# The first MLP matrix by Strassen's seven half products, in a fp32 decoder trunk on one core

## The chip, the core and the metric

The kernel runs on one core of a Trainium2 chip. The core has a matrix engine, TensorE (PE in the profile, its weight loads PEld), three engines for elementwise work, VectorE (DVE), ScalarE (ACT) and GpSimd (POOL), and SyncE (SP), which here only issues loads. Each engine works through its own queue in order; they meet at semaphores. Matmuls write to PSUM banks of 512 fp32 columns; everything else lies in SBUF. The metric is the device time of one execution in microseconds (us), as the median of several.

## The reference

A trunk of two layers over 512 tokens of width 1024. Each layer adds a mixer of four branches, then cross attention, then the MLP, which is the part that changes:

```python
def sq_relu_mlp(h, w1, w2):
    return jnp.square(jax.nn.relu(h @ w1)) @ w2
...
    for l in range(DEPTH):
...
        h = rmsnorm(x, norm_mlp[l])
        x = x + sq_relu_mlp(h, mlp_w1[l], mlp_w2[l])
```

`w1` is 1024 x 4096 and `w2` 4096 x 1024, all in fp32.

## The kernel before

**Layout.** Activations lie turned: a tile is 128 features (partitions) by 512 tokens (columns), eight of them for width 1024. `X` is the residual stream, `Hhi`/`Hlo` the normed input. fp32 products are made of three: every operand is split into a high part and a low part (fp32r), and the matmuls are high x high, high x low and low x high.

**Units.** Weights come in units of 256 x 256 numbers: 128 partitions by two row blocks (`k`) by 256 columns. SP loads each unit into a ring of nine places (`WR`, in the trace `w_raw`), when PE has used the unit nine before it. For each unit ACT writes the high part (`feed`, L1327, `w_hi`), then POOL the low part over the raw one in two instructions of 256 columns (L637 and L638, `w_lo`), then PE may use it (`split_ready`). `feed_past(name)` lets ACT go LEAD = 5 units beyond a block.

**Blocks.** A block makes 256 output features from 1024 input features: 4 units, in each 2 output tiles (`reg`) x 2 input tiles (`k`) x 3 matmuls of 512 columns, 48 matmuls in all. Blocks take turns between two sets of two PSUM banks (`G`); a block may start when both banks of the block before last are released: `pe.wait_ge(gemm_free[s], 2 * used)` at the head of `parts`. The reader of a bank releases it with an empty instruction (`dve.nop().then_inc(gemm_free[s], 1)`). Four more banks, `M` (in the trace `mix`), serve the mixer and the attention.

**The MLP.** `up{q}_{c}` is quarter q (of 1024 hidden features), column c (256 of them); `down{q}_{c}` multiplies quarter q by `w2` and adds to `X`. PE's order is up0, up1, down0, up2, down1, up3, down2, down3, four blocks each (`block_order`). DVE reads an `up` bank with relu and the norm factor in one instruction into `gate_t` (the trace shows `gate_t<-gemm,work`, L1835), ACT squares it (L1798) and writes the high part (L1799), DVE the low part (`work_split<-gate_t,work_split`). A `down` bank is added to `X` by DVE (`x_t<-x_t,gemm`, L1826, in `residual`). The hidden quarters lie in `work_split`, in two places in turn (`MHID`). Elementwise steps go through `do`, by which an engine waits for its own last instruction before it starts the next. `factors(2)` makes the norm's factor from a matmul at the end of `up0_0`, so DVE starts on the MLP at 656.1 us in the first layer.

## Time and profile before

| | |
|---|---|
| median of 3 runs (lowest, highest) | 1979.01 us (1978.82, 1979.11) |
| the profiled execution, its span | 1979.01 us, 1977.2 us |
| PE busy | 1954.3 us (99%) |
| DVE, ACT, POOL busy | 959.0 (49%), 913.8 (46%), 1086.8 us (55%) |
| PE clock granted in the 40 slices | 9 or more tenths in all |
| HBM traffic | 95 GB/s over the span |

The page gives busy time by engine, then the span in 40 slices, the chain of work that ended last, and the costliest groups of instructions with their mean durations. The trace of the same execution can be asked for the instructions of a stretch in order of time, for who waited for whom, and for busy time by stretch. Matmuls overlap one another, so their pace is read from the distance of their starts and not from their durations. All times are from the start of the span.

### The profile page before, as it was taken

The page shows a single profiled execution, that of the slowest core. Times are in us where ns is not written, and L with a number is a line of the kernel's source. Part 1 is how long each engine was busy: PE and PEld are TensorE (multiplying, and loading weights), DVE is VectorE, ACT ScalarE, POOL GpSimd, SP SyncE. Part 2 cuts the span into 40 slices and gives each one's busy share as a digit, 9 for nine tenths or more (in the row PEclk, how much of TensorE's full clock was granted, in tenths as well). Part 3 has the DMA queues.
Part 4 walks back from the last instruction along what each step waited for, and adds up shares of the span by engine and source line. Part 5 has one row for each costly group of instructions (what it writes and reads, how often), then busy time and mean ns, then how long its engine had stood idle before and what let it go on. Part 6 is the DMA issues. An engine that isn't in the chain of part 4 may idle for free.

```text
span 1977.2 us, 30720 instructions
## 1 busy us (share of the span) xinstructions
PE 1954.3 (99%) x11859; PEld 1619.5 (82%) x11859; DVE 959.0 (49%) x1430; ACT 913.8 (46%) x1560; POOL 1086.8 (55%) x1356
## 2 busy tenths in 40 slices
PE   7999999999999999999999999999999999999998
PEld 6778788888888888888887877888798888888887
DVE  5887778856153321211258787786631532211212
ACT  6754645345454542333355546353554544333323
POOL 5565564946835454546464555368585445545451
PEclk9999999999999999999999999999999999999999
DMA  6323333333422333333333233233343233333331
GB/s 188 110 74 86 81 81 87 91 104 112 142 86 81 97 97 96 96 96 98 99 97 81 70 86 81 75 91 86 118 136 110 75 95 97 96 96 97 98 99 70
DMA packets 197262, 190.72 MB, mean 96 GB/s; under 512 B 23738, under 2 KB 190204, under 8 KB 196732
## 3 DMA queue, kind: packets, MB, share of 16 engines
q1 hardware_dynamic: 196252, 186.66, 32.5%
q8 instruction: 94, 1.54, 0.3%
q10 hardware_dynamic: 864, 2.10, 0.3%
q14 instruction: 52, 0.43, 0.1%
HBM read 184.51 MB, written 3.15 MB: 95 GB/s over the span
## 4 chain that ended last, share of the span: by engine, by line
PE 95%; ACT 2%; DVE 2%; issue 0%; DMA 0%; POOL 0%; SPq 0%; DVEq 0%; ACTq 0%
PE gemm L644 87%; PE mix L644 7%; DVE work L1826 1%; ACT w_hi L1327 1%; PE mix L1223 0%; DVE h_lo L1835 0%; DVE work L1835 0%; DMA work<-in_norm_mix_dram 0%; DVE gate_t L1835 0%; PE mix L885 0%; ACT work L1492 0%; PE mix L1119 0%; ACT work_split L1485 0%; DVE work L2217 0%; ACT work L1447 0%
## 5 line engine op out<-in xcount | busy, mean ns | idle before, releaser
L637 POOL TENSOR_TENSOR w_lo<-w_raw,w_hi 128x256 fp32r<-128x256 f32 x676 | 567.2, 839 | 862.3 <-ACT w_hi L1327 861.9
L644 PE MATMUL gemm<-work_split,w_hi 128*128 128x512 f32 (+1 forms) x2064 | 604.2, 377 | 2.8 <-ACTq L1423 2.8
L638 POOL TENSOR_TENSOR w_lo<-w_raw,w_hi 128x256 fp32r<-128x256 f32 x676 | 571.3, 845 | 0.0
L644 PE MATMUL gemm<-h_hi,w_hi 128*128 128x512 f32 x1440 | 568.6, 395 | 1.1 <-DVE h_lo L1835 1.1
L644 PE MATMUL gemm<-h_lo,w_hi 128*128 128x512 f32 x1440 | 560.9, 389 | 0.0
L644 PE MATMUL gemm<-h_hi,w_lo 128*128 128x512 f32 x1440 | 560.8, 389 | 0.0
L1327 ACT ACTIVATE w_hi<-w_raw 128x512 fp32r<-128x512 f32 x676 | 384.7, 623 | 232.2 <-DMA w_raw<-in_mlp_w_dram 186.2
L644 PEld LDWEIGHTS gemm<-work_split,w_hi 128*128 128x128 f32 x2064 | 378.6, 188 | 74.2 <-ACTq L1423 3.7
L644 PE MATMUL gemm<-work_split,w_lo 128*128 128x512 f32 (+1 forms) x1032 | 388.0, 376 | 0.0
L644 PEld LDWEIGHTS gemm<-h_hi,w_hi 128*128 128x128 f32 x1440 | 270.3, 188 | 65.7 <-issue 6.6
L644 PEld LDWEIGHTS gemm<-h_hi,w_lo 128*128 128x128 f32 x1440 | 270.3, 188 | 57.1
L644 PEld LDWEIGHTS gemm<-h_lo,w_hi 128*128 128x128 f32 x1440 | 270.5, 188 | 55.0 <-issue 1.0
L1826 DVE TENSOR_TENSOR x_t<-x_t,gemm 128x512 f32<-128x512 f32 x96 | 66.0, 687 | 356.6 <-PE gemm L644 355.6
L644 PEld LDWEIGHTS gemm<-work_split,w_lo 128*128 128x128 f32 x1032 | 194.3, 188 | 35.4
L1835 DVE SCALAR_TENSOR_TENSOR gate_t<-gemm,work 128x512 f32<-128x512 f32 x64 | 44.3, 692 | 183.7 <-PE gemm L644 166.8
L1798 ACT ACTIVATE gate_t<-gate_t 128x512 f32<-128x512 f32 x64 | 40.5, 632 | 190.9 <-DVE gate_t L1835 190.9
L1826 DVE TENSOR_TENSOR work<-work 128x512 f32<-128x512 f32 (+5 forms) x134 | 120.4, 899 | 14.1 <-ACT work L1528 6.5
L1422 ACT ACTIVATE gate_t<-gemm 128x512 f32<-128x512 f32 x52 | 31.1, 599 | 141.1 <-PE gemm L644 140.7
L644 PEld LDWEIGHTS mix<-work 64*64 64x64 f32 (+4 forms) x3136 | 76.9, 129 | 17.7 <-issue 14.4
L1835 DVE SCALAR_TENSOR_TENSOR work_split<-gate_t,work_split 128x512 fp32r<-128x512 f32 x64 | 45.4, 710 | 88.9 <-ACT work_split L1799 88.9
L644 PE MATMUL mix<-work 64*64 64x64 f32 (+8 forms) x3136 | 84.2, 231 | 0.9 <-DVE work L1835 0.6
L644 PE MATMUL gemm<-w_hi,work_split 128*128 128x512 f32 x192 | 66.1, 398 | 1.5 <-POOL w_lo L638 1.5
(318 smaller groups left out, 1643.6 us busy)
## 6 DMA issues: line engine op xcount, KB each, us to landing
w_raw<-in_mlp_w_dram SPq DMA_DIRECT2D x256, 256.0 KB, 2.7
w_raw<-in_w_in_dram SPq DMA_DIRECT2D x208, 256.0 KB, 2.7
w_raw<-in_xattn_w_kv_dram SPq DMA_DIRECT2D x64, 256.0 KB, 3.0
w_raw<-in_w_branch_dram SPq DMA_DIRECT2D x32, 256.0 KB, 2.6
w_raw<-in_w_out_dram SPq DMA_DIRECT2D x32, 256.0 KB, 2.6
w_raw<-in_xattn_w_q_dram SPq DMA_DIRECT2D x32, 256.0 KB, 2.8
w_raw<-in_xattn_w_o_dram SPq DMA_DIRECT2D x32, 256.0 KB, 2.7
w_raw<-in_w_in_dram SPq DMA_DIRECT2D x32, 128.0 KB, 4.1
```

Source lines behind the costliest of these rows:

```text
L637: pool.tensor_tensor(lo[:, 0:half], raw[:, 0:half], hi[:, 0:half].bitcast(F32), ALU.subtract)
L638: pool.tensor_tensor(lo[:, half:], raw[:, half:], hi[:, half:].bitcast(F32), ALU.subtract).then_inc(split_ready, 1)
L644: return pe.matmul(o, w, a, start=start, stop=stop, skip_group_check=True)
L1327: act.activation(hi, raw, ACT.Copy).then_inc(split_hi, 1)
L1422: do(act.activation(t[:, b, :], G[s][b][:, :], ACT.Tanh, scale=0.5), th_ready)
L1798: do(act.activation(UPX[1], UPX[0], ACT.Square), up_a)
L1826: do(dve.tensor_tensor(o, a, b, op), s)
L1835: do(dve.scalar_tensor_tensor(out=o, in0=a, scalar=sc, in1=b, op0=op0, op1=op1), s)
```

## The change

The first quarter `up0` stays as it was. The blocks of quarters 1 to 3 become `up_sums`: in each unit, the weights are four 128 x 128 pieces (two input tiles by two output tiles), and the input is four pieces of 256 tokens (two tiles by FIRST and SECOND half of the tokens). The 2 x 2 product of such pieces takes eight products; here it takes seven, of sums and differences of the pieces (Strassen's identity in Winograd's form). Each product is three matmuls of 256 columns, accumulated over the four units in seven halves of the four `M` banks.

- The sums of the input are made once a layer by DVE during `up0` (`turned_sums`, `turned_low`, with ACT's `turned_hi`), for all four pairs of tiles.
- The sums of the weights are made by DVE for each unit (`weight_sums`, `sums_low`; ACT's high part in `feed`). One of them is written over its raw unit.
- The seven products are put together by DVE in `products_out`; then ACT does relu, square and the high part, DVE the low part (`hidden_low`). The norm's factor is now in the turned input.
- `up` and `down` blocks alternate from `up1_0` on: `up1_0, down0_0, up1_1, down0_1, ...`, and `down3` at the end.
- The hidden quarters 1 and 3 now lie in `Hhi`/`Hlo`.
- `gemm_free` becomes one semaphore for each bank, and a block waits for its second bank only when it comes to it. S5's semaphores are merged by engine; the order there stays.

```diff
-    order += ups[0] + ups[1] + downs[0] + ups[2] + downs[1] + ups[3] + downs[2] + downs[3]
+    order += ups[0]
+    for q in range(1, 4):
+        for c in range(4):
+            order += [ups[q][c], downs[q - 1][c]]
+    order += downs[3]
...
-                if used:
-                    pe.wait_ge(gemm_free[s], 2 * used)
...
+                        if used and un == 0 and reg * 2 % nt == 0:
+                            pe.wait_ge(gemm_free[s][reg * 2 // nt], used)
...
+                def up_sums(q, c):
+
+                    s, used = psum_set(f"up{q}_{c}")
+                    for b in range(2):
+                        pe.wait_ge(gemm_free[s][b], used)
+                    u0 = first_unit(f"up{q}_{c}")
+                    for j in range(4):
+                        u = u0 + j
+                        pe.wait_ge(split_ready, u + 1)
+                        pe.wait_ge(*of_layer(ws_split, sum_unit(u % NUNIT) + 1))
+                        if (q, c) == (1, 0):
+                            pe.wait_ge(*of_layer(h_ready, 24 + j + 1))
...
+                        for n, (o, (w_hi, w_lo), (t_hi, t_lo), opens) in enumerate((
+                                (M[0][:, FIRST], w(0), t(0, FIRST), True), (M[0][:, SECOND], ws(1), tx(1), False),
+                                (M[1][:, FIRST], w(2), t(1, FIRST), True), (M[1][:, SECOND], ws(2), t(1, SECOND), False),
+                                (M[2][:, FIRST], w(3), tx(2), True), (M[2][:, SECOND], ws(0), t(0, SECOND), False),
+                                (M[3][:, FIRST], w(1), tx(0), True))):
+                            mm(o, w_hi, t_hi, start=opens and j == 0, stop=False)
+                            mm(o, w_hi, t_lo, start=False, stop=False)
+                            i = mm(o, w_lo, t_hi, start=False, stop=j == 3)
...
             def feed(upto):
 
                 for u in range(fed[0], min(upto, ALL_UNITS)):
-                    act.wait_ge(raw_in[u % RING], COME[u])
+                    d = sum_unit(u % NUNIT)
+                    if d is None:
+                        act.wait_ge(raw_in[u % RING], COME[u])
+                    else:
+                        act.wait_ge(*of_layer(ws_ready, d + 1))
+                        act.activation(SWhi[d % 4], SWraw[d % 4], ACT.Copy)
...
+                for t, (q, c) in enumerate(SUM_STEPS):
+                    ahead = first_unit("up{}_{}".format(*SUM_STEPS[t + 1])) if t < 11 else first_unit("down3_0")
+                    if t < 11:
+                        feed(ahead + 3)
+                    s, used = psum_set(f"up{q}_{c}")
+                    act.wait_ge(gemm_done[s], 2 * used + 2)
+                    do(act.activation(UPX[0][:, FIRST], M[0][:, FIRST], ACT.Copy), up_a)
+                    feed(ahead + 4)
+                    for b in range(2):
+                        act.wait_ge(*of_layer(up_v, n + 1))
+                        y = MHRAW[q % 2][:, 2 * c + b, :]
+                        do(act.activation(y, y, ACT.Relu))
+                        do(act.activation(y, y, ACT.Square))
+                        do(act.activation(MHID[q % 2][0][:, 2 * c + b, :], y, ACT.Copy), uphi)
+                        n += 1
+                    if t < 11:
+                        feed(ahead + 8)
...
+                def turned_sums(j):
+
+                    for k in (2 * j, 2 * j + 1):
+                        stt(TMraw[:, k, :], X[:, k, :], col("norm_mlp", k), R(32)[:, 0, :], ALU.mult, ALU.mult)
...
+                def weight_sums(u):
+
+                    dve.wait_ge(raw_in[u % RING], COME[u])
+                    d = sum_unit(u % NUNIT)
+                    if d >= 4:
+                        wait_used(dve, u - 8)
+                    a11, a21, a12, a22 = (WR[:, u % RING, i * P:(i + 1) * P] for i in range(4))
+                    s1, s2, s4 = (SWraw[d % 4][:, i * P:(i + 1) * P] for i in range(3))
+                    tt(s1, a21, a22, ALU.add)
+                    tt(s2, s1, a11, ALU.subtract)
+                    tt(a21, a11, a21, ALU.subtract)
+                    tt(s4, a12, s2, ALU.subtract, ws_ready)
...
+                for c in range(4):
+                    s, used = psum_set(f"up0_{c}")
+                    if c == 3:
+                        for j in range(4):
+                            weight_sums(ahead + j)
+                            if j:
+                                sums_low(ahead + j - 1)
+                        sums_low(ahead + 3)
+                    for b in range(2):
+                        dve.wait_ge(gemm_done[s], 2 * used + b + 1)
+                        if n:
+                            dve.wait_ge(*of_layer(up_a, n))
+                        stt(UPX[0], G[s][b][:, :], 0.0, R(32)[:, 0, :], ALU.max, ALU.mult, up_v)
+                        dve.nop().then_inc(gemm_free[s][b], 1)
+                        if n in TURNS:
+                            turned_low(TURNS.index(n))
+                        n += 1
+                        if n in TURNS:
+                            turned_sums(TURNS.index(n))
+                        hidden_low(0, c, b, UPX[1])
```

On DVE before, at the end of `up1` and the start of `down0`: the reader of each bank (`gate_t<-gemm,work`) and the low part of the hidden tile take turns, and the `down` blocks stand together.

```order
L1835 SCALAR_TENSOR_TENSOR gate_t<-gemm,work 128x512
L1835 SCALAR_TENSOR_TENSOR work_split<-gate_t,work_split 128x512
L1835 SCALAR_TENSOR_TENSOR gate_t<-gemm,work 128x512
L1835 SCALAR_TENSOR_TENSOR work_split<-gate_t,work_split 128x512
L1826 TENSOR_TENSOR x_t<-x_t,gemm 128x512 x8
```

On DVE after, in `up0`: column 2's second bank, then the first units of the weight sums (the rows `w_raw`; `gate_rows` is their high part), which stand ahead of column 3's first bank.

```order
L1923 SCALAR_TENSOR_TENSOR gate_t<-gemm,work 128x512
L1923 SCALAR_TENSOR_TENSOR work_split<-work,work_split 128x1024
L1923 SCALAR_TENSOR_TENSOR work_split<-work,merged_split 128x768
L1923 SCALAR_TENSOR_TENSOR work_split<-gate_t,work_split 128x512
L1914 TENSOR_TENSOR work<-w_raw 128x128
L1914 TENSOR_TENSOR work<-work,w_raw 128x128
L1914 TENSOR_TENSOR w_raw<-w_raw 128x128
L1914 TENSOR_TENSOR work<-w_raw,work 128x128
```

Twenty instructions of weight sums (four units of four sums and one low part) have moved between the reads of the third and the fourth column. The same engine later, in one pair of an `up_sums` and a `down` block after: it ends two units' sums, puts the products together, does the fourth unit, the low parts of the hidden tiles (`h_lo`) and the two residual additions.

```order
L1923 SCALAR_TENSOR_TENSOR work_split<-work,gate_rows 128x384
L1914 TENSOR_TENSOR gate_t<-gate_t,mix 128x256
L1914 TENSOR_TENSOR h_raw<-gate_t,mix 128x256 x2
L1914 TENSOR_TENSOR h_raw<-h_raw,mix 128x256
L1914 TENSOR_TENSOR gate_t<-gate_t,mix 128x256
L1914 TENSOR_TENSOR h_raw<-mix,gate_t 128x512
L1914 TENSOR_TENSOR s_phases<-w_raw 128x128
L1914 TENSOR_TENSOR s_phases<-s_phases,w_raw 128x128
L1914 TENSOR_TENSOR w_raw<-w_raw 128x128
L1914 TENSOR_TENSOR s_phases<-w_raw,s_phases 128x128
L1923 SCALAR_TENSOR_TENSOR work_split<-work,gate_rows 128x384
L1923 SCALAR_TENSOR_TENSOR h_lo<-h_raw,h_hi 128x512
```

Where an `up` and a `down` block had 6 DVE instructions, there are 30 now, and the release of the product banks stands behind `h_raw<-mix,gate_t`. On ACT after, in the same pair: high parts of the sums (`gate_rows<-work`) and of the units alternate, and the copy of a product (`gate_t<-mix`) stands behind three of them.

```order
L1391 ACTIVATE w_hi<-w_raw 128x512
L1878 ACTIVATE gate_t<-mix 128x256
L1389 ACTIVATE gate_rows<-s_phases 128x384
L1391 ACTIVATE w_hi<-w_raw 128x512
L1883 ACTIVATE h_raw<-h_raw 128x512
L1884 ACTIVATE h_raw<-h_raw 128x512
L1885 ACTIVATE h_hi<-h_raw 128x512
```

Before, ACT had only the square and the high part of a tile between its units; the four units of the next `down` block now follow the second tile.

## Rows read from the trace of the kernel before

**Rows 1.** The page: busy time and instructions by engine; shares of the last chain.

```profile
PE 1954.3 (99%) x11859; PEld 1619.5 (82%) x11859; DVE 959.0 (49%) x1430; ACT 913.8 (46%) x1560; POOL 1086.8 (55%) x1356
...
PE 95%; ACT 2%; DVE 2%; issue 0%; DMA 0%; POOL 0%; SPq 0%; DVEq 0%; ACTq 0%
...
L644 PEld LDWEIGHTS gemm<-h_hi,w_hi 128*128 128x128 f32 x1440 | 270.3, 188 | 65.7 <-issue 6.6
```

**Rows 2.** What PE waited for: total us, times, longest us.

```profile
PE gemm L905 <- DMA work<-in_norm_mix_dram: 7.0, 1, 7.0
PE gemm L644 <- ACTq L1423: 2.8, 2, 1.4
```

**Rows 3.** Timeline of PE at `down0_0`: start us, duration us, engine, line, names, count.

```profile
728.37 0.39 PE L644 MATMUL gemm<-h_hi,w_lo 128*128 128x512 f32 x1
...
730.64 0.61 PE L644 MATMUL gemm<-work_split,w_hi 128*128 128x512 f32 x2
```

**Rows 4.** Timeline of DVE, the reads of `up0_0`, `up0_1` and `up0_2`.

```profile
656.08 0.69 DVE L1835 SCALAR_TENSOR_TENSOR gate_t<-gemm,work 128x512 f32<-128x512 f32 x1 [7.89 <-ACT work L1359]
...
664.25 0.69 DVE L1835 SCALAR_TENSOR_TENSOR gate_t<-gemm,work 128x512 f32<-128x512 f32 x1 [2.54 <-PE gemm L644]
...
675.13 0.69 DVE L1835 SCALAR_TENSOR_TENSOR gate_t<-gemm,work 128x512 f32<-128x512 f32 x1 [4.39 <-PE gemm L644]
```

**Rows 5.** Busy time in `up0`: us, PE, PEld, DVE, ACT, POOL, clock, DMA share.

```profile
643.60:687.10 43.50, 43.50 (x191) 35.67 (x190) 14.20 (x19) 20.80 (x35) 22.98 (x32) 1.00 0.36 99
```

**Rows 6.** Timeline of PE in the attention's keys, matmuls of 256 columns.

```profile
485.17 0.28 PE L644 MATMUL gemm<-work_split,w_lo 128*128 128x256 f32 x1
...
485.53 0.28 PE L644 MATMUL gemm<-work_split,w_lo 128*128 128x256 f32 x1
```

**Rows 7.** Timeline of ACT at `gate2_3`, the two banks that `out0` waits for.

```profile
416.99 1.31 ACT L1422 ACTIVATE work<-gemm 128x512 f32<-128x512 f32 x2
```

**Rows 8.** Groups of DVE by shape: busy us, mean ns, idle before.

```profile
L1826 DVE TENSOR_TENSOR x_t<-x_t,gemm 128x512 f32<-128x512 f32 x96 | 66.0, 687 | 356.6 <-PE gemm L644 355.6
...
L1835 DVE SCALAR_TENSOR_TENSOR keys_lo<-gemm,work_split 128x256 fp32r<-128x256 f32 x16 | 6.8, 425 | 30.5 <-ACT work_split L1729 30.2 <-DVE keys_lo L1835 0.3
...
L1960 DVE TENSOR_TENSOR work<-work 128x1024 f32<-128x1024 f32 x2 | 2.5, 1226 | 0.1
...
L1826 DVE TENSOR_TENSOR work<-s_phases 128x128 f32<-128x128 f32 x8 | 2.3, 291 | 0.3
...
L1826 DVE TENSOR_TENSOR s_small<-s_small 128x8 f32<-128x8 f32 x10 | 1.7, 167 | 0.3
```

**Rows 9.** Timeline of DVE behind a release, and of ACT in `feed` and behind DVE.

```profile
611.09 0.75 DVE L1835 SCALAR_TENSOR_TENSOR h_lo<-x_t,params_all,h_hi 128x512 fp32r<-128x512 f32 x1 [0.16 <-DVE x_t L1826]
...
646.15 2.19 ACT L1327 ACTIVATE w_hi<-w_raw 128x512 fp32r<-128x512 f32 x4
...
656.87 0.63 ACT L1798 ACTIVATE gate_t<-gate_t 128x512 f32<-128x512 f32 x1 [0.88 <-DVE gate_t L1835]
```

**Rows 10.** Groups of ACT by shape: busy us, mean ns, idle before.

```profile
L1428 ACT ACTIVATE work<-work 128x1024 f32<-128x1024 f32 x12 | 12.7, 1062 | 27.0 <-DVE work L1826 26.9
...
L1447 ACT ACTIVATE work<-mix 128x256 f32<-128x256 f32 x16 | 6.2, 385 | 5.9 <-PE mix L644 5.5
```

**Rows 11.** Timelines of DVE and POOL where both work, at three sizes.

```profile
143.06 0.64 DVE L1826 TENSOR_TENSOR s_tmp<-s_pw 128x8 f32<-128x8 f32 x1
...
260.82 1.72 DVE L1826 TENSOR_TENSOR work<-work,consts_sb 128x256 f32<-128x256 f32 x2
...
1004.10 1.11 DVE L1835 SCALAR_TENSOR_TENSOR gate_t<-x_t,params_all,work 128x512 f32<-128x512 f32 x1
1004.63 1.19 POOL L638 TENSOR_TENSOR w_lo<-w_raw,w_hi 128x256 fp32r<-128x256 f32 x1
1005.25 1.12 DVE L1835 SCALAR_TENSOR_TENSOR h_lo<-gate_t,h_hi 128x512 fp32r<-128x512 f32 x1
```

**Rows 12.** Busy time at the end of the span, columns as in rows 5.

```profile
1972.00:1974.00 2.00, 0.00 (x0) 0.00 (x0) 0.12 (x1) 0.69 (x1) 0.00 (x0) 0.50 1.02 406
```

More of the change, by code:

```diff
@@ L1287, in turned, with down @@
+                def down(q, c):
+                    hb = MHID[q % 2]
+                    gemm(f"down{q}_{c}", lambda k: hb[0][:, k, :], lambda k: hb[1][:, k, :],
+                         ready=uplo if c == 0 else None, ready_at=8 * q)
+                for q, c in SUM_STEPS:
+                    up_sums(q, c)
+                    down(q - 1, c)
+                for c in range(4):
+                    down(3, c)
             def turned(k, ts):
@@ new lines, in _ @@
+                feed_past("up1_0")
+                feed(first_unit("down0_0") + 4)
+                for t, (q, c) in enumerate(SUM_STEPS):
[6 more added lines that the diff above has]
+                    feed(ahead + 4)
+                    for b in range(2):
+                        act.wait_ge(*of_layer(up_v, n + 1))
+                        y = MHRAW[q % 2][:, 2 * c + b, :]
[5 more added lines that the diff above has]
+                        feed(ahead + 8)
@@ L2557, in _ @@
+                residual("down2_3")
+                for c in range(4):
+                    residual(f"down3_{c}", norm=3)
+                if now[0] < DEPTH - 1:
+                    unscaled_low("norm_mix", 7, 1)
+                    add_squares(3, 7, 8)
             dve.wait_ge(p_act, PRO_ACT + 2)
```

239 lines of the change are left out of this document (142 added, 97 removed).

## The prediction, made before the changed kernel was run

> **What bounds the kernel now.** I read the engine shares and the chain first: TensorE (PE) is busy 99% of the span, and 95% of the chain that ended last is PE [rows 1]. The list of what PE waited for comes next: past the 7.0 us at the start no entry is over 2.8 us, and that one, on ACT's L1423, is a step that frees a PSUM bank before `out0` [rows 2]. So the time is the matmuls' spacing times their number. In the MLP 512-column matmuls start every 0.227 us (ten between 728.37 and 730.64, where `down0_0` starts) [rows 3]; a block is 48 of them, 10.88 us, which is also the distance between DVE's reads of successive blocks, 664.25 and 675.13 [rows 4]. In the first 43.5 us of the MLP DVE is busy 14.2 us and POOL 23.0 (53%), at full clock [rows 5]. DVE has much room, and the change spends it.
>
> **What is removed.** A summed block is 4 units x 7 products x 3 = 84 matmuls of 256 columns. The trace has such a stretch: three start every 0.36 us (485.17, 485.53, 485.89), 0.120 each, each with its own weight load (as many loads as matmuls, rows 1) [rows 6]. A block then takes 84 x 0.120 = 10.08 us in place of 10.88: 0.80 saved, 12 blocks a layer, two layers: 19.2 us. Seven eighths of the work gives 7% and not 12.5%, because a half-width matmul costs 0.120 and not 0.113. The separate release of the two PSUM banks helps in one place: `out0` waits 1.4 us in each layer for both banks of `gate2_3`, and ACT reads them one after the other, both in 1.31 us [rows 2, 7]. Half of that, 0.7, comes off in each layer: 1.4 us (none at worst, 2.8 at best). The renamed S5 semaphores order the same instructions: nothing.
>
> **What is added, on DVE.** Prices, without anybody in the way: 128 columns 0.29, 256 columns 0.425, 512 columns 0.69, 1024 columns 1.23 [rows 8]; so 384 columns 0.56 and 768 columns 0.97 by interpolation. The next instruction starts 0.03 later; behind a bank release 0.16 later (the idle time before `h_lo` at 611.09) [rows 9]. ACT: 512 columns 0.63, its spacing in `feed` 2.19/4 = 0.55 [rows 9], 256 columns from PSUM 0.385, 1024 columns 1.06 [rows 10]; so a 384-column copy holds the queue 0.44. ACT starts 0.10 after DVE's signal (656.08 + 0.69 = 656.77, ACT at 656.87) [rows 4, 9].
>
> **DVE and POOL in each other's way.** Where both read SBUF, both get longer. In rows 11, 512-column DVE instructions follow each other every 1.145 us in place of 0.72, with one POOL instruction of 1.19 between each two (22.98/32 = 0.72 in the MLP, rows 5); 256-column ones take 0.86 in place of 0.425; and an 8-column one 0.64 in place of 0.17 [rows 8, 11]. The surcharge is the same at every size, 0.42 to 0.47, once for each DVE instruction that meets one of POOL. I take 0.43 for 128 columns, since its neighbours on both sides (8 and 256) show it. DVE instructions that read PSUM don't pay: `x_t<-x_t,gemm` stays at 0.69 over all 96 [rows 8]. Of the 30 DVE instructions of a pair, 22 read only SBUF, 16 of them of 128 columns. The Trainium skill (SBUF — State Buffer, section "SBUF: two separate sides") calls this an exclusive lock on which the loser fully blocks for the whole instruction. By that a meeting would cost POOL's whole 0.72 and the pair below 25.1 us, some 60 us more in all; the rows agree that both wait, and speak against that size.
>
> **Steady state: one pair (`up_sums`, `down`).** PE needs 10.08 + 10.88 = 20.96 us. DVE's program for it, from one release of the product banks to the next, is one chain, since DVE and ACT hand work to and fro:
> - fourth unit's sums 4 x 0.32 = 1.28; then ACT: 0.10 + 0.44 + 0.55 (`feed`) + 0.66 + 0.66 + 0.66 (relu, square, copy) = 3.07; until ACT's second such three 1.98; last `hidden_low` 0.72
> - two residuals 2 x 0.84 = 1.68; three units' sums 12 x 0.32 = 3.84; one low part 0.59
> - ACT again: 0.10 + 0.44 + 0.55 + 0.42 = 1.51 (the copy of M[0] stands behind `feed(ahead + 3)` in its queue)
> - the products' six additions, from PSUM: 5 x 0.455 + 0.69 + two releases 0.25 = 3.2
>
> Sum 17.9. Meetings: ACT splits the four `down` units right after its last copy, so POOL's 8 instructions for them (0.72 each) begin with the residuals; two pass there, six meet the sums, and the 4 of the first two summed units follow: 10 of 13 meet. 17.9 + 10 x 0.43 = 22.2. Bounds: none meets, 17.9; all 13, 23.5. Since PE may not begin the next `up_sums` before the product banks are free, PE stops 22.2 - 20.96 = 1.2 us a pair (0 to 2.5). `up1_1` to `up3_3` are 11 such starts: 13.2 us a layer. Once late, DVE waits for nobody but ACT, so the loads, which hang on PE's progress, are early. Behind DVE's waits stand its residuals, for which nobody is in a hurry (the `down` banks have a whole pair).
>
> **The entry, from `up0` to `up1_0`.** DVE adds to each column of `up0` two scalings, four sums and two low parts. A column: 2 x 0.83 + 2 x 0.78 + 4 x 0.455 + 2 x 0.72 + 1.26 + 1.00 and 0.6 waiting for ACT's 1.06 + 0.87 = 9.3, under 10.88. The first begins at 656.1 with POOL idle: 665.4, when the bank of `up0_1` has waited since 664.25 [rows 4]. In the next two, 53% of ten SBUF instructions meet POOL (+2.2): 11.5 each, to 688.4. Now the four units of `up1_0`: 16 x 0.32 + 4 x 0.59 = 7.5, six meetings 2.6, waits for the splits 0.4: 698.9. Only then `up0_3` is read, and the last turned sums: 9.3 - 0.7 = 8.6, one meeting 0.4, to 707.9. PE comes to `up1_0` at 687.1 (730.64 - 4 x 10.88); it stops there for the first weight sums until 692.3 (688.4 + 2.56 + 1.0 + 0.3), and before its fourth unit, wanted at 694.7, for the turned sums until 708.1. Together 13.4 us a layer. Bounds: without any meeting DVE starts from 675.1 + 9.3, and the same sums end at 701.0: 6.3; with every one, 19.
>
> **Sum.** A layer: -9.6 + 13.4 + 13.2 = +17.0; two: +34.0; the bank release -1.4: +32.6. The profiled execution took 1979.01 (its span 1977.2 and 1.8 around it), which is the median itself: 2011.6 us. From eight meetings a pair (stop 0.3) to twelve (2.1) it is 1993 to 2030.
>
> **Rivals.**
> - **POOL and DVE pass each other** (faster). If the meetings fall away, the pair's 17.9 fits into 20.96, the product banks are free before PE asks, and only the entry's 6.3 stays: 1979.0 + 2 x (6.3 - 9.6) - 1.4 = 1971. Speaks for it: POOL is busy only half the time. Against: ACT hands POOL its 8 instructions just when DVE comes to its smallest ones, and all rows with both at work show the surcharge. It decides at (20.96 - 17.9)/0.43 = 7 meetings: below, no stop. With the entry at 13.4 and no stop it gives 1985.
> - **Everything is hidden**: 1979.0 - 19.2 - 1.4 = 1958. It would take an entry that DVE does in its spare time; against it stands that `up0_3` is read only after 20 instructions of weight sums.
> - **The clock falls** in the entry's stops of 5 and some 8 us. The profile has one fall: at the very end, where PE has nothing left to do, the granted clock is 0.50, 1.2 in place of 2.4 GHz [rows 12]. The same in the entry would double the matmuls that follow; 8 us at the lower level lose 4, of which the next stop (1.2) swallows a part: 3 a layer, 2017. The Trainium skill (TensorE: Matmul & The Clock Gate, Part 1) has the same rule, that an idle array goes to half its rate; the row agrees on the level.
> - **The short matmuls are slower in this order**, because seven bank halves and more weights alternate: if the weight load's own 0.188 [rows 1] were the limit, a block would take 15.8 us and the kernel 1979 + 24 x 4.9 = 2097, or somewhat more. Against: the stretch in rows 6 has one load per matmul and keeps 0.120.
>
> **Chances.** Forecast 0.62 (1993 to 2030); the clock with it 0.13; POOL and DVE pass 0.14 (1971 to 1985); all hidden 0.06; slower matmuls or still more meetings 0.05. The range 1978 to 2030 leaves out about 0.17. What a measurement can tell from no change is about 0.2%, 4 us: faster (below 1975) 0.19, same 0.04, slower 0.77.
>
> **What the changed profile would show.** Matmuls of 256 columns every 0.120 us; two stops of PE before `up1_0` and inside it, released by DVE's low parts; then a stop of about 1.2 us before each `up` of the second and third quarter, its releaser DVE's last product addition (or its queue); DVE's 128-column sums at two lengths, 0.29 and 0.72, with a mean near 0.55; DVE busy nearly all of the MLP; PE's busy share down to some 97%. I am wrong if the 128-column sums are mostly 0.29, if PE runs through from `up1_1` on, or if DVE waits for `gemm_done` in each pair: then it isn't DVE's chain that sets the pace. The entry's term is wrong if `up1_0` doesn't stop before its last unit.

## The result, and the profile of the changed kernel

The changed kernel takes **2011.07 us** (median, 2010.56 to 2011.16), the kernel before 1979.06 beside it: a ratio of **1.016, with an interval of 1.0148 to 1.0173**. The forecast was 2011.6, slower. The profiled execution took 2010.56, its span is 2008.8.

The page of the changed kernel, busy time and instructions by engine and the shares of the last chain (against [rows 1]):

```profile
PE 1949.5 (97%) x12723; PEld 1651.8 (82%) x12723; DVE 1323.9 (66%) x2070; ACT 1004.6 (50%) x1744; POOL 1105.1 (55%) x1356
...
PE 66%; DVE 21%; ACT 9%; issue 2%; DVEq 0%; DMA 0%; POOL 0%; SPq 0%; ACTq 0%
```

PE was 95% of the chain and is 66%; DVE and ACT, 4% together, are 30%. PE's busy time fell by only 4.8 us, since it counts matmuls that ran slower in two stretches of each layer (below).

What PE waited for, in the whole span (total us, times, longest), against [rows 2]. `DVEq` and `ACTq` are those engines' queues: the empty instructions by which they release a bank (L2663 is the release of the product banks).

```profile
PE mix L675 <- DVEq L2663: 15.9, 19, 0.9
PE mix L675 <- POOL w_lo L669: 11.1, 2, 5.5
PE mix L675 <- DVE work_split L1923: 11.0, 2, 5.7
...
PE gemm L675 <- ACTq L1487: 1.4, 2, 0.7
```

The first three are new: one stop for weight sums and one for turned sums in each layer, and 19 short ones, ten in the first layer and nine in the second. They sum to 38.0 us; the rest of the loss is in matmuls that ran slower behind the long stops, and in what the brackets leave out (below). The last row answers to the 2.8 us on ACT's L1423: 1.4 is left, as forecast.

PE's timeline in layer 0: the last matmul of `up0`, where `up1_0` starts, its fourth unit, then `up1_1`, `up1_2`, `up1_3` and `up3_3` (in brackets the idle time and who ended it):

```profile
686.00 0.39 PE L675 MATMUL gemm<-h_hi,w_lo 128*128 128x512 f32 x1
691.92 0.55 PE L675 MATMUL mix<-work_split,w_hi 128*128 128x256 f32 x1 [5.53 <-POOL w_lo L669]
...
707.41 0.77 PE L675 MATMUL mix<-work_split,w_hi 128*128 128x256 f32 x2 [5.22 <-DVE work_split L1923]
...
722.59 0.40 PE L675 MATMUL mix<-work_split,w_hi 128*128 128x256 f32 x2
...
744.55 0.36 PE L675 MATMUL mix<-work_split,w_hi 128*128 128x256 f32 x1 [0.82 <-DVEq L2663]
...
766.61 0.36 PE L675 MATMUL mix<-work_split,w_hi 128*128 128x256 f32 x1 [0.86 <-DVEq L2663]
...
943.15 0.36 PE L675 MATMUL mix<-work_split,w_hi 128*128 128x256 f32 x1 [0.85 <-DVEq L2663]
```

A pair of blocks lasts 766.61 - 744.55 = 22.06 us, and (943.15 - 744.55)/9 = 22.07 on the mean, where PE needs 20.96. The bracket shows 0.85, but the step from one start to the next is 1.11 too long; I count with the step. `up1_1` starts at 722.59 without a stop. `up1_0` could have started one spacing behind the last matmul of `up0`, at 686.00 + 0.23 = 686.23, and `up1_1` at 686.23 + 10.08 + 10.88 = 707.19, so the entry cost 15.4 us. From there to `up3_3` are ten pairs: 943.15 - 722.59 - 10 x 20.96 = 11.0. The first layer loses 26.4. The second, counted the same way, loses 16.4 in the entry (`up1_0` wanted at 1673.89, `up1_1` at 1711.27) and 9.6 in nine late pairs, 26.1.

The 687.10 of the prediction is a time of the trace before, which runs 0.9 later at this place. DVE's first read of `up0_0` shows it: 656.08 there [rows 4], and here

```profile
655.19 0.69 DVE L1923 SCALAR_TENSOR_TENSOR gate_t<-gemm,work 128x512 f32<-128x512 f32 x1 [7.88 <-ACT work L1423]
```

So times of the entry are compared from this read on.

DVE's timeline for one pair:

```profile
797.57 0.47 DVE L1914 TENSOR_TENSOR work<-w_raw 128x128 f32<-128x128 f32 x1 [0.22 <-DVE x_t L1914]
798.07 0.71 DVE L1914 TENSOR_TENSOR work<-work,w_raw 128x128 f32<-128x128 f32 x1
...
802.54 0.71 DVE L1914 TENSOR_TENSOR work<-w_raw,work 128x128 f32<-128x128 f32 x1
803.29 0.56 DVE L1923 SCALAR_TENSOR_TENSOR work_split<-work,gate_rows 128x384 fp32r<-128x384 f32 x1
803.88 0.29 DVE L1914 TENSOR_TENSOR work<-w_raw 128x128 f32<-128x128 f32 x1
...
804.54 0.77 DVE L1914 TENSOR_TENSOR w_raw<-w_raw 128x128 f32<-128x128 f32 x1
805.34 0.71 DVE L1914 TENSOR_TENSOR work<-w_raw,work 128x128 f32<-128x128 f32 x1
...
815.18 0.69 DVE L1923 SCALAR_TENSOR_TENSOR work_split<-work,work_split 128x512 fp32r<-128x512 f32 x1 [2.50 <-ACT work_split L1885]
...
817.17 0.69 DVE L1923 SCALAR_TENSOR_TENSOR work_split<-work,work_split 128x512 fp32r<-128x512 f32 x1 [0.71 <-ACT work_split L1885]
817.90 1.52 DVE L1914 TENSOR_TENSOR x_t<-x_t,gemm 128x512 f32<-128x512 f32 x2
819.64 0.47 DVE L1914 TENSOR_TENSOR work<-w_raw 128x128 f32<-128x128 f32 x1 [0.22 <-DVE x_t L1914]
```

From 797.57 to 819.64 are 22.07 us, PE's own period, and in it DVE waits for nobody but ACT and itself; PE, the loads and POOL end none of its waits. Of the sums in the first two groups seven last 0.71 (798.07 to 802.54), one 0.47; then two of 0.29, one 0.77, one 0.71: 9.4 meetings with POOL at 0.43, where 10 were forecast. The four sums behind the products last 0.29. DVE's two waits for ACT's hidden parts are 2.50 and 0.71, and one of 0.89 for ACT's copy of the first product lies before the additions.

The granted clock in the entry, by windows (us, PE, PEld, DVE, ACT and POOL busy, clock, DMA share, GB/s), against [rows 5, 12]:

```profile
687.10:692.00 4.90, 0.08 (x1) 0.11 (x1) 4.52 (x12) 2.08 (x4) 2.01 (x3) 0.87 0.17 54
692.00:696.00 4.00, 4.00 (x19) 4.00 (x20) 3.76 (x8) 1.04 (x2) 2.37 (x4) 0.50 0.00 0
...
704.00:708.00 4.00, 0.59 (x3) 0.62 (x4) 3.32 (x4) 3.87 (x8) 0.92 (x2) 0.55 0.06 21
708.00:712.00 4.00, 4.00 (x22) 3.96 (x22) 3.83 (x6) 1.16 (x4) 4.00 (x6) 0.60 0.00 0
712.00:722.50 10.50, 10.50 (x48) 8.69 (x47) 8.81 (x17) 2.81 (x6) 5.92 (x8) 1.00 0.31 101
```

Behind each of the two long stops the clock is at its lower level for some microseconds: 19 matmuls in the 4 us from 692 on, where full speed gives 33.

### The profile page after: what moved, and what is told of

Its sections match the earlier page's. It is cut to its first block, busy times and chain, and to the rows that moved or that the text cites. A ratio compares the mean times of both kernels' runs of the same rounds, so it can differ in the third digit from the quotient of the medians.

```text
span 2008.8 us, 33630 instructions
## 1 busy us (share of the span) xinstructions
PE 1949.5 (97%) x12723; PEld 1651.8 (82%) x12723; DVE 1323.9 (66%) x2070; ACT 1004.6 (50%) x1744; POOL 1105.1 (55%) x1356
## 4 chain that ended last, share of the span: by engine, by line
PE 66%; DVE 21%; ACT 9%; issue 2%; DVEq 0%; DMA 0%; POOL 0%; SPq 0%; ACTq 0%
PE gemm L675 57%; DVE work L1914 9%; PE mix L675 8%; DVE w_raw L1914 3%; DVE work_split L1923 2%; ACT w_hi L1391 2%; DVE h_raw L1914 1%; DVE x_t L1914 1%; ACT gate_rows L1389 1%; DVE s_phases L1914 1%; DVE work L1923 1%; DVE gate_t L1914 1%; ACT h_raw L1884 1%; ACT h_hi L1885 1%; DVE h_lo L1923 1%
## 5 line engine op out<-in xcount | busy, mean ns | idle before, releaser
L675 PE MATMUL gemm<-h_hi,w_hi 128*128 128x512 f32 x1312 | 518.9, 395 | 1.1 <-DVE h_lo L1923 1.1
L675 PE MATMUL gemm<-h_lo,w_hi 128*128 128x512 f32 x1312 | 511.1, 390 | 0.0
L675 PE MATMUL gemm<-h_hi,w_lo 128*128 128x512 f32 x1312 | 511.0, 390 | 0.0
L675 PE MATMUL gemm<-work_split,w_hi 128*128 128x512 f32 (+1 forms) x1552 | 447.4, 373 | 1.4 <-ACTq L1487 1.4
L675 PEld LDWEIGHTS gemm<-work_split,w_hi 128*128 128x128 f32 x1552 | 281.8, 189 | 51.9 <-ACTq L1487 2.2
L675 PE MATMUL gemm<-work_split,w_lo 128*128 128x512 f32 (+1 forms) x776 | 288.7, 372 | 0.0
L675 PE MATMUL mix<-work_split,w_hi 128*128 128x256 f32 (+1 forms) x544 | 125.4, 295 | 37.9 <-DVEq L2663 15.9
L1914 DVE TENSOR_TENSOR work<-work 128x256 f32<-128x256 f32 (+5 forms) x160 | 136.8, 855 | 15.3 <-ACT work L1592 6.5
L675 PEld LDWEIGHTS mix<-work_split,w_hi 128*128 128x128 f32 x544 | 92.8, 196 | 47.4 <-DVEq L2663 23.4
L675 PE MATMUL mix<-work_split,gate_rows 128*128 128x256 f32 x504 | 105.9, 289 | 0.0
```

The lines of the kernel that those rows point to most:

```text
L675: return pe.matmul(o, w, a, start=start, stop=stop, skip_group_check=True)
L1914: do(dve.tensor_tensor(o, a, b, op), s)
```

## The experiments

Each is the changed kernel with one edit, except the two on the kernel before and the three attempts at the end, which combine several.

### TensorE's own part

```diff
-                    s1, s2, s4 = (SWraw[d % 4][:, i * P:(i + 1) * P] for i in range(3))
+                    s1, s2, s4 = (SWraw[d % 4][:, i * P:i * P + 8] for i in range(3))
...
-                        ws = lambda n: (SWhi[j][:, n * P:(n + 1) * P], SWlo[j][:, n * P:(n + 1) * P])
+                        ws = w
```

and the same for the low parts, the turned sums and ACT's copies of them.

> The changed kernel with all matmuls in number, width and order, but every sum and low part that the change added to DVE, and ACT's copies of them, only 8 columns wide; TensorE takes the weights themselves and the hidden activations in place of the sums, so the products are not those of the identity, and ACT's square there is a scaled copy. It prices TensorE's own part. Theory (a summed block is 84 x 0.120 = 10.08 us, the rest is DVE's lateness): the chain falls by 16 x 0.12 + 4 x 0.4 = 3.5 to 18.6 a pair, and the entry is done in spare time: no stops, 1979.0 - 19.2 - 1.4 = 1958, up to 1962 with small stops. Rival (short matmuls that alternate banks and weights are slower, or the blocks' starts stop for another reason): 1970 or more, without the DVE stops.

Measured: 1958.94 us (0.9898, 0.9883 to 0.9913), and the list of PE's waits within the MLP is empty. So 84 half-width matmuls in the identity's order do take 10.08 us. The changed kernel lies 52.1 above this floor; the 26.4 and 26.1 of its trace sum to 52.5, the same within half a microsecond.

### The bank releases, and the alternation

The kernel before with the bank releases (and the merged S5 semaphores):

```diff
-                if used:
-                    pe.wait_ge(gemm_free[s], 2 * used)
+                        if used and un == 0 and reg * 2 % nt == 0:
+                            pe.wait_ge(gemm_free[s][reg * 2 // nt], used)
```

> The kernel before with one part of the change alone: each of the two PSUM banks of a pair has its own release, and the S5 stage's semaphores are merged. Whole computation. Prediction's term: out0 waits 0.7 a layer in place of 1.4, so 1.4 us off the kernel before, 1977.4 from 1978.8; the wait on ACT's L1423 before out0 is halved in the list of PE's waits. Rival: the first matmuls of a block find other reasons to wait, or the added wait instruction costs PE time at every block: 1978.8 or more, up to 1981.

and with the blocks' order besides:

```diff
-    order += ups[0] + ups[1] + downs[0] + ups[2] + downs[1] + ups[3] + downs[2] + downs[3]
+    order += ups[0]
+    for q in range(1, 4):
+        for c in range(4):
+            order += [ups[q][c], downs[q - 1][c]]
+    order += downs[3]
```

> The kernel before with the separate bank releases and with the `up` and `down` blocks alternating as in the changed kernel, but all products in full: no sums, no turned sums. Whole computation. Theory (the alternation costs nothing by itself, all of the loss hangs on the sums): as the bank releases alone, 1977.4. Rival (the alternation itself makes stops, by the loads of another matrix, by the residuals' place or by POOL): 1980 or more, and stops in the MLP.

Measured: 1977.63 (0.9992, 0.9983 to 1.0002) and 1977.55 (0.9993, 0.9984 to 1.0003), beside 1979.06. Both intervals hold 1, so the time alone doesn't prove the gain of 1.4; the list of waits has the halved wait in both kernels. Of the first:

```profile
PE gemm L644 <- ACTq L1427: 1.4, 2, 0.7
```

The alternation costs nothing that can be measured.

### POOL's share of the pair

```diff
+                wide = 8 if UNITS[u % NUNIT][0].startswith("down") else half
-                pool.tensor_tensor(lo[:, 0:half], raw[:, 0:half], hi[:, 0:half].bitcast(F32), ALU.subtract)
+                pool.tensor_tensor(lo[:, 0:wide], raw[:, 0:wide], hi[:, 0:wide].bitcast(F32), ALU.subtract)
```

> The changed kernel, with POOL's two instructions for each unit of a `down` block cut to 8 columns each (TensorE takes the high part of these weights where it took the low part, so the low part of the down weights is left out of the result). Nothing else is touched: DVE and ACT run the same instructions in the same order. Theory (POOL and DVE in each other's way make the pair too long): six of the pair's ten meetings were with these instructions; at 0.43 each the chain falls from the measured 22.07 us a pair by 2.6 to 19.5, under TensorE's 20.96. The ten stops a layer (1.11 each beyond TensorE's need) go, about 22 us in all, and some 0.5 to 1 a layer in the entry with them: 1986 to 1990. The 128-column sums behind the residuals go back to 0.29. Rival (the chain is long by itself, and the double length of the sums is not POOL's doing): 2011, the stops stay and the sums keep both lengths.

Measured: 1989.97 (1.0056, 1.0041 to 1.0071). Within the MLP of layer 0 PE waits twice, and never from `up1_1` on:

```profile
PE mix L676 <- DVE work_split L1924: 6.1, 1, 6.1
PE mix L676 <- POOL w_lo L670: 5.5, 1, 5.5
```

The sums that last 0.71 above are now like this one:

```profile
790.15 0.29 DVE L1915 TENSOR_TENSOR work<-w_raw 128x128 f32<-128x128 f32 x1 [0.22 <-DVE x_t L1915]
```

DVE and ACT do the same work in the same order, so without POOL's part the pair fits. The entry did not get cheaper, as expected it should by 0.5 to 1: its second stop ends 52.2 us after DVE's first read, as in the changed kernel.

### The residual out of the chain

```diff
-                    if t:
-                        residual("down{}_{}".format(SUM_STEPS[t - 1][0] - 1, SUM_STEPS[t - 1][1]))
...
                         sums_low(ahead + 2)
+                    residual(f"down{q - 1}_{c}")
                     hidden_low(q, c, 0, MHRAW[q % 2][:, 2 * c, :])
```

> The changed kernel, whole computation; in DVE's order the residual of `down{q-1}_{c}` (two additions of 512 columns) stands behind the fourth unit's sums, where DVE waits for ACT's relu, square and copy, and no longer at the head of the pair. Theory (one chain through DVE and ACT from release to release of the product banks sets the pair): the two additions with their releases, 2 x 0.84 = 1.68, leave the chain: 22.07 - 1.68 = 20.4, under 20.96, so TensorE stops no more before `up1_2` to `up3_3`: 2011.1 - 2 x 10 x 1.11 = 1989, 1987 to 1993 if the meetings with POOL fall otherwise. Rival (the pair is set by DVE's whole busy time, or by the loads or POOL's split): the work is the same, so 2011, or a stop that only changes its releaser.

Measured: 1999.64 (1.0104, 1.0089 to 1.0119), half of what was expected. The stops are still there, and shorter (nine of 0.25 in the first layer, seven in the second); a pair lasts 21.47. Its DVE timeline after ACT's last hidden part:

```profile
815.31 0.80 DVE L1914 TENSOR_TENSOR work<-w_raw 128x128 f32<-128x128 f32 x1
...
821.37 0.98 DVE L1923 SCALAR_TENSOR_TENSOR work_split<-work,gate_rows 128x384 fp32r<-128x384 f32 x1
```

The 1.68 did leave the chain. But the residuals read PSUM and pay nothing to POOL; they had been the cover under which POOL's first two instructions passed. Now sums stand there: 11 of the 12 sums and the first low part meet POOL, 12 meetings in place of 9.4. 22.07 - 1.68 + 2.6 x 0.43 = 21.5, the measured 21.47.

### ACT's hidden part first

```diff
-                    feed(ahead + 4)
                     for b in range(2):
+                        if b:
+                            feed(ahead + 4)
                         act.wait_ge(*of_layer(up_v, n + 1))
```

> The changed kernel, whole computation; in ACT's order the relu, square and copy of the first of a block's two hidden parts come before the copies for the weights' fourth unit, which wait for DVE's last sums. Theory (the pair is one chain through DVE and ACT, in which DVE waits 2.50 and 0.71 for ACT's hidden parts): ACT begins the first part at once after DVE's fourth product addition, 1.98 earlier than now against DVE's last step, so the last `hidden_low` comes about 2.0 earlier and the chain falls from 22.07 to 20.1, under 20.96, with the same meetings with POOL, since these begin behind ACT's last copy as before. No stops from `up1_1` on: 2011.1 - 22 = 1989, 1986 to 1993. Rival (DVE's own work sets the pair): the time goes into another wait, and 2005 or more is left.

Measured: 1989.76 (1.0056, 1.0039 to 1.0073), as expected. DVE's timeline:

```profile
770.27 0.47 DVE L1915 TENSOR_TENSOR work<-w_raw 128x128 f32<-128x128 f32 x1 [0.22 <-DVE x_t L1915]
...
790.36 0.46 DVE L1915 TENSOR_TENSOR work<-w_raw 128x128 f32<-128x128 f32 x1 [0.22 <-DVE x_t L1915]
```

20.09 from pair to pair, while DVE is still late from the entry: the wait of 2.50 is gone, and the sums between residuals and products meet POOL as before. One changed place in ACT's queue removes all steady stops. DVE's own work fits; the chain did not.

### The entry's list made longer

```diff
                         stt(TMraw[:, k, :], X[:, k, :], col("norm_mlp", k), R(32)[:, 0, :], ALU.mult, ALU.mult)
+                        stt(TMraw[:, k, :], X[:, k, :], col("norm_mlp", k), R(32)[:, 0, :], ALU.mult, ALU.mult)
```

> The changed kernel, whole computation, with the two scalings that open each `turned_sums` done twice (two more DVE instructions of 512 columns in each of the four columns of `up0`, 0.69 + 0.03 each, more where they meet POOL). Theory (the entry is set by DVE's list from column 2 on): column 2's pair delays the first weight sums by 1.4 to 2.3, and so the first stop (5.53) by as much; column 3's delays the last turned sums by as much again: 2.9 to 4.6 a layer, 2017 to 2020 in all. Columns 0 and 1 have slack and add at most 1 a layer more. Rival (the entry waits for loads, POOL's low parts or ACT): no change, 2011.

Measured: 2023.03 (1.0221, 1.0204 to 1.0238): 12.0 more, 6.0 a layer, above the 2.9 to 4.6 expected. All four columns count: 4 x 2 x 0.72 = 5.8. From its first read at 655.92 DVE never waits for PE in the entry, only for ACT, 0.6 at a time. The slack I gave to columns 0 and 1 isn't there; PE even stops for 2.20 inside `up0_3`. The rival's "no change" is excluded.

### Fewer, wider sums

```diff
+                    a11, a21, a12, a22 = (WR[:, r:r + 2, i * P:(i + 1) * P] for i in range(4))
...
-                        weight_sums(ahead)
-                        weight_sums(ahead + 1)
+                        weight_sums_two(ahead)
```

> The changed kernel, whole computation, with the weight sums of the first two units of a block made at once, as four DVE instructions of 256 columns in place of eight of 128 (except where the two units lie at the two ends of the ring). The same elements are added. Theory (DVE pays once for each instruction that meets POOL, at any size): eight instructions of 0.745 each are replaced by four of 0.87, 2.5 less, part of which the later sums give back because they now meet POOL, up to 1.3: the chain falls from 22.07 to between 19.6 and 20.9, under TensorE's 20.96 or at it; in the entry 1 to 2 a layer less: 1985 to 1991. Rival (the surcharge grows with the size, as if DVE and POOL shared the port by the element): four instructions of 1.4, no gain, 2008 or more.

Measured: 2003.61 (1.0124, 1.0111 to 1.0138), 12.6 above the theory's range, yet well under the rival's. The timeline settles why:

```profile
797.41 0.84 DVE L1914 TENSOR_TENSOR work<-w_raw 128x256 f32<-128x256 f32 x1 [0.68 <-DVE x_t L1914]
...
802.06 1.13 DVE L1923 SCALAR_TENSOR_TENSOR work_split<-work,gate_rows 128x384 fp32r<-128x384 f32 x1 [1.18 <-ACT w_hi L1391]
```

The price is as the theory has it, 0.84 for 256 columns where 128 take 0.71: the surcharge doesn't grow with DVE's columns. But ACT can copy the first unit's sums only when both units' are done, and the low part behind them waits 1.18 for that copy, and the low part met POOL besides (1.13). Part of the gain went into a wait that the small instructions had covered. The entry, expected 1 to 2 us shorter, is 0.5 longer: its second stop ends 52.8 us after DVE's first read.

### POOL's instruction made longer

```diff
+                if UNITS[u % NUNIT][0].startswith(("up", "down")):
+                    pool.tensor_tensor(lo, raw, hi.bitcast(F32), ALU.subtract).then_inc(split_ready, 1)
+                    continue
```

> The changed kernel, whole computation, with POOL making the low part of each MLP unit in one instruction of 512 columns in place of two of 256 (6 in place of 12 a pair of blocks; about 1.3 to 1.4 each when alone, as estimated from 0.72 for 256). It tells what a meeting costs. Theory of the prediction (0.43 once for each DVE instruction that meets POOL, whatever its size; it would then be whatever POOL's size too): at most 6 or 7 meetings a pair, 17.9 + 6.5 x 0.43 = 20.7, under 20.96, so no stops: 1988 to 1991. Rival (a DVE instruction that meets POOL waits out what is left of POOL's instruction, so that DVE and POOL take turns): 6 meetings of some 0.43 + 0.6 = 1.0 each, 17.9 + 6.2 = 24.1 a pair, stops of 3.1, 2050; half way, with the same total for POOL's columns, 22 to 22.5 a pair and 2011 to 2020.

Measured: 2025.41 (1.0236, 1.022 to 1.0251), 22.55 a pair (815.40 - 792.85). The prediction's "once per meeting, whatever the size" falls. POOL's and DVE's timelines:

```profile
795.40 1.30 POOL L668 TENSOR_TENSOR w_lo<-w_raw,w_hi 128x512 fp32r<-128x512 f32 x1 [4.81 <-ACT w_hi L1394]
```

```profile
801.73 0.89 DVE L1917 TENSOR_TENSOR work<-w_raw 128x128 f32<-128x128 f32 x1 [0.22 <-DVE x_t L1917]
802.65 1.26 DVE L1917 TENSOR_TENSOR work<-work,w_raw 128x128 f32<-128x128 f32 x1
...
806.87 1.54 DVE L1926 SCALAR_TENSOR_TENSOR work_split<-work,gate_rows 128x384 fp32r<-128x384 f32 x1
808.45 1.27 DVE L1917 TENSOR_TENSOR work<-w_raw 128x128 f32<-128x128 f32 x1
```

A 128-column sum that meets POOL now takes 1.26, one of 384 columns 1.54: 0.97 and 0.98 more than alone, where it was 0.42 and 0.41 with POOL's short instruction. POOL's instruction grew from 0.74 to 1.30, by 0.56, and the surcharge by the same 0.55. It is POOL's instruction, as long as it takes alone, less some 0.32, for both sizes of DVE's. (Alone, because POOL gets longer too: the 1.19 of [rows 11] is its 0.74 beside 512-column DVE instructions, whose surcharge was still 0.43.) Fewer meetings (4.6 by these rows: 0.60 + 3 x 0.97 + 0.98 = 4.5 us) cost more in all: 17.9 + 4.5 = 22.4, measured 22.55.

### Three attempts at a faster kernel

The first puts `down` before `up` in each pair, so that `down0_0` covers the first weight sums, and adds the merged sums and ACT's new order:

```diff
-            order += [ups[q][c], downs[q - 1][c]]
+            order += [downs[q - 1][c], ups[q][c]]
```

> An attempt at a faster kernel, whole computation, from three findings: (1) the `down` block of a pair comes before its `up` block, so that `down0_0` stands between `up0_3` and `up1_0`, and DVE reads `up0_3` before it makes the first weight sums; (2) the sums of a block's first two units are made at once, as 256-column instructions; (3) ACT takes the first hidden part before the fourth unit's copies (where a quarter ends, both parts). Theory: the steady stops go (chain 22.07 - 2.0 - 1.7, under 20.96), and the entry's two stops of together 14.5 a layer shrink to 3 to 7, since the sums have the 10.9 us of `down0_0` as cover; at the three quarter ends `down` directly follows the last `up` and may stop 0 to 1.5 for the last hidden part: 1958.9 + 2 x 6 = 1971, 1963 to 1977, below the kernel before. Rival (entry set by the loads or by POOL's and ACT's queues): a stop of 10 or more a layer stays, 1980 to 1990.

Measured: 1991.7 (1.0066, 1.0051 to 1.0081), 15 above the range. The steady stops are gone, but others have come, of which I had priced only a part:

```profile
699.97 0.50 PE L675 MATMUL gemm<-work_split,w_hi 128*128 128x512 f32 x1 [3.32 <-DVE work_split L1923]
...
704.92 0.36 PE L675 MATMUL mix<-work_split,w_hi 128*128 128x256 f32 x1 [1.16 <-POOL w_lo L669]
...
787.95 0.50 PE L675 MATMUL gemm<-h_hi,w_hi 128*128 128x512 f32 x1 [1.37 <-DVE h_lo L1923]
...
789.94 0.79 PE L675 MATMUL gemm<-h_hi,w_hi 128*128 128x512 f32 x1 [1.02 <-DVE h_lo L1923]
```

`down` now follows directly on the block whose hidden part it needs. In the entry that part is ready at 699.92, since it hangs on all of DVE's list. At the quarter's end DVE makes the next block's sums before it reads the finished products (the first at 783.26). The stops of this layer come to 9.0, and behind three of them the granted clock is low again:

```profile
700.00:704.00 4.00, 3.75 (x9) 2.43 (x9) 2.66 (x5) 1.98 (x4) 1.03 (x2) 0.57 0.00 0
...
788.00:792.00 4.00, 2.98 (x8) 2.11 (x9) 1.86 (x5) 1.77 (x4) 0.00 (x0) 0.66 0.15 50
792.00:800.00 8.00, 8.00 (x49) 7.52 (x48) 2.50 (x3) 2.41 (x5) 7.30 (x10) 0.74 0.22 67
```

That is 4 x 0.43 + 4 x 0.34 + 8 x 0.26 = 5.2 us of full speed. The second layer differs: its stops come to 10.1, and the clock takes 3.3 (0.61 for 4 us from 1677 on, 0.57 for 4 us from 1854 on). At the place of the last two rows it stays at 1.00 there, behind stops of 1.76 and 1.03. Each of the seven brackets is 0.16 short of the step, a matmul's 0.39 less the spacing of 0.23, so the two layers lose about 15.3 and 14.5. The profiled execution, 1990.11, lies 31.2 above the floor; 1.4 stay unexplained.

The second leaves the blocks' order as changed and computes `up1_0` in full; the identity begins at `up1_1`, and ACT takes the hidden part first:

```diff
-        SUM_STEPS = [(q, c) for q in range(1, 4) for c in range(4)]
+        SUM_STEPS = [(q, c) for q in range(1, 4) for c in range(4)][1:]
+        FULL_STEPS = [(0, 0), (0, 1), (0, 2), (0, 3), (1, 0)]
...
+                gemm("up1_0", *H)
+                down(0, 0)
                 for q, c in SUM_STEPS:
```

> Second attempt at a faster kernel, whole computation: the changed kernel with ACT's first hidden part before the fourth unit's copies (as in the run before last), and with `up1_0` computed in full, as eight half products, so that the identity begins at `up1_1`. Theory (the entry's loss is DVE's list, which has begun at 655.2 and runs without a gap; it only needs cover): the list without weight sums ends the four columns at about 697, `up1_0`'s own reads at 702, and the first sums are ready at 705, before the 708.9 at which TensorE comes to `up1_1`, and the turned sums long before; the last unit's sums at about 712 against 716. No stop in the entry, none after it (chain 20.1), the clock stays: 1979.0 - 1.4 - 2 x 11 x 0.80 = 1960, 1958 to 1966. Rival (the sums of a first block stop TensorE wherever they begin, for example by ACT's and POOL's queues): 5 or more a layer remain, 1970 or more.

Measured: **1969.6 (0.9953, 0.9939 to 0.9966), faster than both kernels**, though 4 above the range. The clock stays. In the first layer three small stops are left up to the start of `up1_1` and one behind it (in the second, two and one); the largest:

```profile
711.70 0.48 PE L676 MATMUL mix<-work_split,w_hi 128*128 128x256 f32 x2 [1.35 <-POOL w_lo L670]
```

I had left out that DVE, in a full block, waits for ACT between each read and its low part:

```profile
703.27 1.13 DVE L1924 SCALAR_TENSOR_TENSOR h_lo<-gate_t,h_hi 128x512 fp32r<-128x512 f32 x1 [1.36 <-ACT h_hi L1867]
...
706.54 0.69 DVE L1924 SCALAR_TENSOR_TENSOR h_lo<-gate_t,h_hi 128x512 fp32r<-128x512 f32 x1 [1.41 <-ACT h_hi L1867]
```

The third puts the first two units' sums into these two waits, and lets ACT feed two more units before it waits for turned sums:

```diff
+                        if q:
+                            weight_sums(first_unit("up1_1") + b)
                         hidden_low(q, c, b, UPX[1])
...
                         if n in TURNS:
+                            feed(min(first_unit(f"up{q}_{c}") + 4 + LEAD + 2, first_unit("up1_1")))
                             turned_hi(TURNS.index(n))
```

> Third attempt at a faster kernel, whole computation: the second one (first block in full) with two idle stretches of its entry filled. DVE makes the weight sums of the first two units of `up1_1` while it waits 1.36 and 1.41 us for ACT's square and copy in `up1_0`, and ACT copies two more units of weights before it waits 4.54 us for the turned sums. Theory (in the second attempt TensorE stops 0.26 and 0.85 in the last full blocks for low parts that ACT's queue hands to POOL late, 1.35 before `up1_1` for its first weight sums, and 0.70 before `up1_2` because DVE is still late): these go, 3.2 a layer; at best 1969.6 - 6 = 1964, 1963 to 1967. Rival (the sums in the gaps meet POOL and delay the reads of `up1_0`, or the copies come before their weights have landed): no gain or a loss, 1969 to 1973.

Measured: **1965.51 us (0.9933, 0.992 to 0.9945)**, 13.3 under the kernel before. PE's waits within the MLP of layer 0 are

```profile
PE mix L676 <- DVE work_split L1927: 0.9, 1, 0.9
PE mix L676 <- DVEq L2667: 0.7, 1, 0.7
```

Above the floor of 1958.94 it loses 3.3 a layer: 0.8 for the block in full and 2.3 around these two stops, counted by step (1.04 before `up1_1`, then 1.30 beyond the 20.96 to `up1_2`). DVE ends both; what would remove them was not tried.

## Why the prediction was right, and where not

The way and the two mechanisms, entry and chain, are the ones the runs isolate. That the time came within 0.6 us is in part luck, since two errors cancelled: for the first layer the prediction gave the entry 13.4 and the later pairs 13.2, and the trace has 15.4 and 11.0, so that 26.6 stands against 26.4. Point by point:

- **Matmuls.** Forecast -19.2 and -1.4; together 20.6; the floor lies 19.8 under the kernel before that ran beside it (1978.77), the bank releases 1.4. Right.
- **Chain.** Forecast 17.9 + 10 meetings = 22.2; measured 22.07 with 9.4 meetings. That it is a chain and not DVE's load shows in ACT's new order (20.09 with DVE's work untouched); that the meetings with POOL bring it above PE's 20.96, in POOL's short instructions. The threshold holds too: with the chain under 20.96 the stops vanish, and 21.47 leaves short ones. Late pairs were 10 in the first layer and 9 in the second, not 11, since the entry took their place: 11.0 and 9.6, forecast 13.2.
- **The price of a meeting.** The right number, from rows in which POOL always had the same instruction; the statement on record is too wide. The surcharge doesn't depend on DVE's size, and does on that of POOL's instruction. I also wrote that the rows speak against the Trainium skill (SBUF — State Buffer, section "SBUF: two separate sides"), by which the loser blocks for the whole instruction. They spoke only against the full 0.72. The run with the longer instruction agrees in kind, since what DVE pays grows with POOL's instruction, and not in full: it is POOL's duration alone less 0.32.
- **Entry.** Forecast stops until 692.3 and 708.1, which is 36.2 and 52.0 after DVE's first read; measured 691.92 and 707.41, 36.7 and 52.2 after it. `up1_1` was to start at 708.1 + 2.52 + 10.88 + 1.2 = 722.7, 66.6 after the read, and starts 67.4 after it. The two brackets, 5.53 and 5.22, sum to 10.7 and not 13.4, for between them three units ran at the lower clock and took up what DVE was late anyway. That DVE's list sets it from its first instruction is shown by the doubled scalings. The first stop is ended by POOL's low part of the first unit, not by a low part of DVE's as forecast: DVE's first four sums end at 688.77, ACT's two copies at 689.91 and POOL's two instructions at 691.71, 0.6 behind DVE's own low part (691.13).
- **The clock.** It fell, as the rival said, behind both stops, and I had given that 13%. Its price was mis-sized: 3 more a layer were forecast, and in the first layer it is some 0.6. The first fall cost nothing that shows: PE was still 5.22 early at the fourth unit. The second slowed the fourth unit and the start of `down0_0` (707.41 to 722.59 are 15.2 in place of 13.4), and these 1.8 took the place of the forecast stop of 1.2 at `up1_1`. In the second layer the same stretch took 16.2, and the stop at `up1_2` went as well. So the forecast and this rival, priced apart, came true together, with one time.
- **All hidden, and short matmuls slower**: both excluded, the one by the stops, the other by the floor.
- The list of what would be seen was right but for "DVE busy nearly all of the MLP": it waits 4.1 us a pair for ACT, which the chain contains and the sentence forgot; and but for the releaser of the first stop.

The loss thus has two separate causes, each enough to eat the gain of 9.6 a layer. Moving two ACT copies (a unit's sums and the unit) removes the steady one; starting the identity one block later removes most of the other, for 0.8.

## What to carry to other kernels

When work moves from the bottleneck to a helper engine, add up the helper's path from one release to the next, its waits for third engines included, and compare that, not its busy share: here DVE's share rose to 66% and it was the limit. Then look at the order in the engine that hands back (ACT): two copies for later work ahead of a result that is wanted now cost 2 us a pair, more than the whole excess of 1.1. New preparation needs cover before its first use; to leave the first block as it was can be cheaper than to prepare for it.

Moving an instruction away can take away a cover: the residuals, which read PSUM, had let POOL pass, and half the gain of moving them went back into meetings.

## What the runs showed of the hardware

- A DVE instruction with two inputs in SBUF that meets POOL's takes longer by POOL's duration alone less 0.32: 0.29 becomes 0.71 beside POOL's 0.74, and 1.26 beside 1.30. With 128-column DVE instructions the two go in step, one of each every 0.745 us from 798.07 on. An addition of 256 columns with one input in PSUM, at 807.53 beside a running POOL instruction, takes 0.42 as it does alone. Long POOL instructions were thus worse for DVE than the same columns in two: 2025.41 against 2011.07.
- Stops of 5 us before or within a block were followed by some 4 us or more at clock 0.50 to 0.60; the 19 short ones, 0.57 to 0.86, left it at full speed. In the first attempt two stops of 1.37 and 1.02, some 2 us apart, were followed by 0.66 and 0.74, and two of 1.76 and 1.03 at the same place of the second layer by 1.00. So the length of a stop alone does not decide it; what does was not tried.
- 84 matmuls of 256 columns, alternating over seven bank halves and each with a weight load of its own, keep 0.120 us: the floor's 1958.94 is what this spacing gives.
